# Projection strips in pairs by seven block products, and the last expert pairs loaded by halves

## The reference

```python
proj = x @ w_in + b_in                       # 1024 -> 6 x 1024
ya = (bg * short_conv(cg * xc)) @ w_conv_out
ys = ssm_branch(us)                          # state scan, 64 groups x 64 states
z = gelu(ys)
glu = z * sigmoid(z @ w_glu + b_glu)
yb = glu @ w_ssm_out
m = sigmoid(ga) * ya + sigmoid(gb) * yb
x = layer_norm(ALPHA * x + m @ w_o)
f = moe_ffn(x)       # router: top 8 of 64 experts in 4 of 8 groups; SwiGLU experts of width 256; one shared expert
x = layer_norm(ALPHA * x + f)
```

## Time and profile before

| | us |
|---|---|
| median of 3 runs | 828.49 (826.7 to 829.38) |
| the profiled execution, own time | 828.15 |
| its span on the core | 826.4 |
| PE busy | 807.5 (98%) |
| DVE busy | 465.6 |
| ACT busy | 162.7 |
| POOL busy | 93.2 |
| HBM to and from | 326 GB/s over the span |

### The profile page before, as it was taken

How to read it: one execution, slowest core, us unless ns; L and a number is a source line. 1 busy time by engine, 2 the same in 40 slices (tenths; PEclk the granted TensorE clock), 3 DMA queues, 4 the chain that set the end, 5 groups by cost and what they waited for, 6 DMA issues and landing times.

```text
span 826.4 us, 11871 instructions
## 1 busy us (share of the span) xinstructions
PE 807.5 (98%) x4275; PEld 504.1 (61%) x4275; DVE 465.6 (56%) x1179; ACT 162.7 (20%) x269; POOL 93.2 (11%) x105
## 2 busy tenths in 40 slices
PE   9999999999999999899999999999999999999994
PEld 7876788888788888544445454454545545444442
DVE  6989899999741367534434443343434334334356
ACT  2210112111221005321212112121212112112115
POOL 1119700000010002100000000000000000000021
PEclk9999999999999999999999999999999999999998
DMA  9433344445489946699999999999999999999961
GB/s 330 152 128 103 124 140 144 153 153 114 152 334 420 404 159 268 216 395 418 424 423 420 427 424 420 426 424 421 425 426 422 425 426 422 426 425 423 422 275 54
DMA packets 43639, 262.08 MB, mean 317 GB/s; under 512 B 9736, under 2 KB 10504, under 8 KB 24528
## 3 DMA queue, kind: packets, MB, share of 16 engines
q1 hardware_dynamic: 38992, 252.87, 76.3%
q0 software_dynamic: 4608, 8.66, 2.8%
HBM read 267.10 MB, written 2.53 MB: 326 GB/s over the span
## 4 chain that ended last, share of the span: by engine, by line
PE 83%; DMA 14%; DVE 2%; ACT 1%; issue 0%; SPq 0%; POOL 0%; ACTq 0%; DVEq 0%; POOLq 0%
PE banks L1219 35%; PE banks L1424 22%; DMA ring<-w_gu 14%; PE banks L1467 10%; PE banks L1391 6%; PE banks L1366 3%; PE banks L1320 1%; PE banks L1234 1%; PE banks L1246 1%; PE banks L1396 1%; PE banks L1439 1%; PE banks L1252 1%; PE banks L1495 0%; ACT cgb L697 0%; DVE cgb L1191 0%
## 5 line engine op out<-in xcount | busy, mean ns | idle before, releaser
L1424 PE MATMUL banks<-high,low 128*64 128x512 f32 x848 | 232.1, 593 | 2.2 <-DMA high<-w_gu 2.2
L1219 PE MATMUL banks<-xT,ring 128*128 128x264 f32 x768 | 176.9, 390 | 0.0
L1132 DVE TENSOR_TENSOR cgb<-cgb,banks 128x264 f32<-128x264 f32 x248 | 90.0, 424 | 137.4 <-PE banks L1391 137.3
L1219 PEld LDWEIGHTS banks<-xT,ring 128*128 128x128 f32 x768 | 145.1, 191 | 30.2 <-issue 5.5
L1424 PEld LDWEIGHTS banks<-high,low 128*64 128x64 f32 x848 | 74.2, 137 | 137.2 <-issue 132.4
L1177 DVE SCALAR_TENSOR_TENSOR y_pair<-banks,sml,y_pair 128x1024 fp32r<-128x1024 f32 x31 | 39.8, 1284 | 121.8 <-ACT y_pair L687 121.8
L532 POOL DMA_INDIRECT low<-x_rows_dram,idx x32 | 31.9, 997 | 427.6 <-DVE idx L1076 423.2
L1424 PE MATMUL banks<-ring,low 128*64 128x512 f32 x176 | 77.5, 593 | 1.3 <-DMA ring<-w_gu 1.3
L1391 PEld LDWEIGHTS banks<-sw,y_pair 128*128 128x128 f32 x496 | 63.0, 188 | 24.9 <-issue 24.3
L1467 PE MATMUL banks<-high,mu 128*64 128x512 f32 x336 | 76.7, 598 | 0.2 <-DVE cgb L1132 0.2
L1391 PE MATMUL banks<-sw,y_pair 128*128 128x264 f32 x496 | 71.1, 293 | 0.0
(11 more groups left out here) (294 smaller groups left out, 856.0 us busy)
## 6 DMA issues: line engine op xcount, KB each, us to landing
high<-w_gu SPq DMA_DIRECT2D x40, 2048.0 KB, 28.0
high<-w_dn SPq DMA_DIRECT2D x42, 1024.0 KB, 23.9
ring<-w_front SPq DMA_DIRECT2D x78, 512.0 KB, 3.3
high<-w_gu SPq DMA_DIRECT2D x28, 1024.0 KB, 10.0
ring<-w_gu SPq DMA_DIRECT2D x8, 2048.0 KB, 32.4
us<-w_dn SPq DMA_DIRECT2D x11, 1024.0 KB, 22.5
ring<-w_gu SPq DMA_DIRECT2D x6, 1024.0 KB, 10.4
bgb<-w_dn SPq DMA_DIRECT2D x6, 1024.0 KB, 22.5
```

Of the source, the lines that this page charges most:

```text
L1132: dve.tensor_tensor(acc[:, n], acc[:, n], psum[:, bank, 0:T], ALU.add).then_inc(added, 1)
L1219: ins = pe.matmul(psum[:, 6 + n % 2, 0:T], ring[:, n % RING, k], rhs[:, k], start=(k == 0), stop=(k == KC - 1))
L1424: ins = pe.matmul(psum[SL * j:SL * j + SL, GU_BANK, :], xg[:, k, SL * j:SL * j + SL], gu[slots[j]][:, k], start=(k == 0), stop=(k == KC - 1))
```

## The change

**Pairs of strips by seven products.** The first two GLU strips (0 and 4) stay as they are (`PLAIN`, `FRONT`). The other 22 are done as 11 *quads*: quad q takes strips n and n + 4 of a projection, that is a 2x2 block product: outputs in two chunks, inputs in two groups of four chunks, tokens in two halves of 132. Instead of eight block products it makes seven, of sums and differences of the blocks (Winograd's form). Each is four matmuls of 132 columns. The sums of weight blocks (`left_sums`, four for each quad, 128x512) are made by POOL, those of the activations (`right_sums`, four for each projection) by DVE, and DVE puts the seven products together (`join`), with a first copy by ACT. A quad that begins a projection (3 and 7) takes the first three of four chunks of products 1 to 5 ahead, since the fourth needs the outcome of the quad before.

**DMA.** Quads have three slots of 1 MB, and a pair's strips are one load of two halves; one piece of expert weights stands behind the strips of each of quads 1 to 9. Scratch for the sums lies where expert slots are, so gate and up of experts 0 and 4 and down of expert 5 are no longer loaded between the strips but at the end of the quads, behind the tenth and the eleventh, and the shared expert's down weights at the seventh quad's end.

**Last pairs by halves.** Visit 30 also waits by halves. For visit 31 the second half of gate and up comes in two parts and the down weights by row halves; the combination of visit 30 and the mean move between the two halves of its gate and up matmuls, DVE adds all eight chunks of it before it multiplies the hidden rows (L1161 of before), and the down projection runs over both column halves for each row half.

The core of the diff, for POOL, ACT, and three places of DVE:

```diff
+                for q in range(len(QUADS)):
...
+                    if q > 1:
+                        pool.wait_ge(products, PRODUCTS * (q - 1))
+                    pool.wait_ge(quad_loaded[q % QUAD_RING], 32 * (q // QUAD_RING + 1))
+                    pool.tensor_tensor(s1, two[:, 0:HC], two[:, HC:KC], ALU.add).then_inc(left_ready, 1)
+                    pool.wait_ge(left_ready, 4 * q + 1)
+                    pool.tensor_tensor(s2, s1, one[:, 0:HC], ALU.subtract).then_inc(left_ready, 1)
+                    pool.tensor_tensor(s3, one[:, 0:HC], two[:, 0:HC], ALU.subtract).then_inc(left_ready, 1)
+                    pool.wait_ge(left_ready, 4 * q + 2)
+                    pool.tensor_tensor(s4, one[:, HC:KC], s2, ALU.subtract).then_inc(left_ready, 1)
...
+                for q in range(len(QUADS)):
+                    if q > 1:
+                        act.wait_ge(joined, q - 1)
+                    act.wait_ge(products, PRODUCTS * q + 1)
+                    act.activation(first_product[:, q % 2], psum[:, 3 * (q % 2) + 2, 0:TH], ACT.Copy).then_inc(first_copied, 1)
+                    if q < FIRST_SSM:
+                        act.wait_ge(joined, q + 1)
+                        for c in (q + 1, q + 1 + HC):
+                            glu_gate(c, xcb[:, c]).then_inc(gated, 1)
...
+                def glu_products(i):
+
+                    dve.tensor_tensor(both(cgb, i), both(us, i), both(xcb, i), ALU.mult).then_inc(glu_ready, 1)
+                    dve.wait_ge(glu_ready, i + 1)
+                    if i == HC - 2:
+                        sum_right(1, cgb, 0, HC - 1)
+                    if i == HC - 1:
+                        sum_right(1, cgb, HC - 1, HC)
...
+                for i in range(HC):
+                    if i >= HC - 2:
+                        sum_weights(i - (HC - 2))
+                    join(FIRST_SSM + i, i)
+                    do(dve.tensor_tensor(both(gbb, i), both(xcb, i), both(gbb, i), ALU.mult))
+                    dve.tensor_tensor(both(bgb, i), both(gbb, i), both(bgb, i), ALU.add).then_inc(m_ready, 1)
+                    dve.wait_ge(m_ready, i + 1)
+                    if i == HC - 2:
+                        sum_right(2, bgb, 0, HC - 1)
+                    if i == HC - 1:
+                        sum_right(2, bgb, HC - 1, HC)
...
-                for n in range(KC - 1):
+                for n in READY_ORDER[:KC - 2]:
                     center(0, r_, n)
...
+                join(len(QUADS) - 1, last, xT)
```

More of the change, by code:

```diff
@@ L44 @@
 RING = 4
+PLAIN = GLU + 2
+FRONT = list(range(GLU + 1)) + [GLU + HC]
+QUADS = [GLU + i for i in range(1, HC)] + [SSM + i for i in range(HC)] + [OUT + i for i in range(HC)]
+FIRST_SSM, FIRST_OUT = HC - 1, 2 * HC - 1
+FIRST_QUADS = (FIRST_SSM, FIRST_OUT)
+TH = T // 2
+PRODUCTS, QUAD_RING = 7, 3
+READY_ORDER = [n + HC * h for n in range(HC) for h in range(2)]
 UNIT = 2
@@ L216, in build @@
         strips_done = sem("strips_done")
+        quad_loaded = [sem(f"quad_slot{i}_loaded") for i in range(QUAD_RING)]
+        left_ready = sem("left_sums_ready")
+        right_ready = sem("right_sums_ready")
+        products = sem("quad_products_done")
+        first_copied = sem("quad_first_product_copied")
+        joined = sem("quad_blocks_joined")
+        gated = sem("glu_gates_ready")
         bank_free = [sem(f"bank{i}_free") for i in range(2)]
@@ L693, in _ @@
                 visit(turns * PER_TURN + 1, 1, last=True)
[L694 removed]
+                squares(1, acc, range(KC))
                 for n in range(KC):
@@ L1157, in visit @@
                         dve.wait_ge(added, before + 1)
-                        for n in range(ADDED_FIRST):
+                        for n in range(KC if last else ADDED_FIRST):
                             add(n, before, CHUNK_BANKS[n])
@@ L1161, in visit @@
                     dve.tensor_tensor(h_sl, sil_sl, psum[:, GU_BANK, F:2 * F], ALU.mult).then_inc(hx_ready, 1)
-                    if before is not None:
+                    if before is not None and not last:
                         for n in range(ADDED_FIRST, KC):
@@ L1287, in _ @@
                         pe.wait_ge(mean_parts, 1)
                         pe.matmul(psum[:, MEAN_BANK[0], 0:T], ones[:], mu[:, 2], start=True, stop=True).then_inc(stat_out, 1)
-                    strip(n, bgb, rhs_ready=m_ready if n == OUT else None)
+                    pe.wait_ge(first_copied, q + 1)
+                    pe.wait_ge(left_ready, 4 * q + 4)
+                    product(bank + 2, TH, s4, end[:, HC:KC])
+                    pe.wait_ge(right_ready, 8 * m + 8)
+                    product(bank + 2, 2 * TH, two[:, HC:KC], t4)
@@ L1291, in logits @@
+                for q in range(len(QUADS)):
+                    if q < FIRST_SSM:
+                        quad(q, 0, us)
+                    elif q < FIRST_OUT:
+                        quad(q, 1, cgb, glu_ready)
+                    else:
+                        quad(q, 2, bgb, m_ready)
                 def logits(first, end):
-                    for k in range(first, end):
-                        pe.wait_ge(centered, k + 1)
+                    for i in range(first, end):
+                        k = READY_ORDER[i]
+                        pe.wait_ge(centered, i + 1)
```

310 lines of the change are left out of this document (215 added, 95 removed).

## The result

The changed kernel takes 844.04 us (median of 4 runs, 842.25 to 848.46); the kernel before took 828.93 in the same series (826.7 to 829.4). The ratio is 1.0203, 95% interval 1.0184 to 1.0222: slower by 15 to 18 us, as forecast (845.7). The profiled execution took 844.83, with a span of 843.1, 16.7 more than before.

A forecast was written before the change was run, and what follows sets the result against it. PE was taken to bound the strips (229.5 to 315.6 us), the stream of expert weights the later stage. Terms -9.0 + 21 + 5.4 - 0.3 = +17.1 on the median 828.5 gave 845.7 us with roundings; range 827 to 850.

The forecast's parts named there:

- The bound: Expert stage: the stream of weights bounds it, so the end moves by as much as the first gated load (339.32).
- Products: PE in the quads: 616 matmuls at 0.1125 us replace 22 strips, 69.3 us for 78.3, so -9.0.
- Turns: Quads: POOL's sums and DVE's operations with two SBUF inputs exclude each other for whole operations, making PE wait: +21 us.
- start: First quads: DVE's right sums alternate with POOL's sums, the first join is late and PE waits in quad 1: 7.3 us.
- GLU to SSM: Passage between these projections: right sums alternate with POOL, so third join and product come late for PE: 4.1 us.
- SSM to OUT: Passage between these projections: DVE's multiplications and sums in turns with POOL, then a weight sum, delay PE: 8.4 us.
- sums of inputs: Eight DVE sums of inputs meet POOL's eight router multiplications, so the mean is late: 1.1 us.
- The rival of the clock: PE's clock falls to 1.2 GHz behind each of three pauses, 3 us each: 850 to 854 us; chance 0.07.
- No exclusion: Rival: POOL and DVE hardly hinder each other, sum -4.3, 824.2 us, faster than before; chance 0.13.
- milder: Rival: exclusion on one side only or DVE first, 7 to 15 us instead of 21: 832 to 840; chance 0.24.
- End of the quads: Behind the last quad: DVE's last join and centerings come late and ACT has one more square: +5.4 us.
- Last visits: Visits 30 and 31: visit 30 starts 1.2 to 1.3 us earlier, visit 31 loses 1.0: sum -0.3 us.

The follow-up runs named there:

- run 1: The changed kernel with POOL's 44 sums of weight blocks left out, strip blocks standing in for them: ratio 1.0006 to the kernel before, 828.9 us.
- run 3: A program of its own, without the kernel's computation, with phases of equal POOL and DVE operations alone and together: a pair of two-input sums every 1.55 us.
- Run 9: The kernel before with only the change to visits 30 and 31 (weights by halves, combination and mean moved): ratio 0.9992, 827.6 us.
- run 8: The changed kernel with POOL's five waits, DVE's work reordered, last pair as plain strips, and loads behind the quads in two steps: ratio 0.9994, 827.2 us.

## Why the prediction was right, step by step

- **The bound.** The gated load moved by 16.8 us and the end by 16.7. Right.
- **Products.** 0.1125 a record and 6.30 us a quad: -9.0 as summed. The bounds above it (0.120, 0.129) were not needed. With the 19.2 of the next point, and a start of the strips 0.3 earlier in this execution (229.18 against 229.52), this gives the +9.9 of PE's end.
- **Turns.** Forecast 21, measured 19.2 over a quad's 6.3 and the mean's matmul, at the forecast places: start 7.3 forecast, 7.3 measured (quads 1 and 2); GLU to SSM 4.1 forecast, 2.7 measured; SSM to OUT 8.4 and 8.9, with 0.3 more in quad 6; sums of inputs 1.1 and nothing. But this agreement is in part luck. A pair of operations costs 1.55 us, not the 1.85 that I put together from whole lengths, so the first join ended at 250.6 and not 253.6 and PE's pause was 4.4 and not 6.2; the first wait of 1.1 for right sums did not come (quad 0 takes 6.4). What filled the term up again is the clock: about 2.6 us in quads 1 and 2 and 2.0 in quad 7 are records at 0.22 us, behind the pauses. So half clock made 4.6 and waiting some 14.6, where the sum had 21 for waiting alone; and of the 14.6 the 2.1 of run 1 are there without POOL, so they are DVE's own backlog and not the turns.
- **The rival of the clock** I priced at 3 us a pause and took for unlikely (0.07). It was the case at all three long pauses, with 2.0 to 2.6 us each; as it came with smaller pauses the time stayed near the forecast. The step that failed is treating turns and clock as alternatives: the forecast was right in what makes the time, and the clock, 7.0 us in all, was missing from the sum.
- **The other rivals.** *No exclusion* falls by runs 1 and 3, *milder* by run 3, where the sums go strictly one after the other. The rule of the Trainium skill (SBUF — State Buffer, "Who interferes with whom") holds in the phases shown in run 3; by it an operation in a two-port mode contends too, which fits the one-input operation in one piece. POOL's operation with one input, in the last section, is where the measurement differs from it.
- **End of the quads.** Forecast 5.4, measured 6.9. The last chunks are ready 4.7 us behind PE's end instead of 0.5, so 4.2 later, where 5.1 was forecast. The second square is 0.3, as forecast. The other 2.4 is half clock until the matmuls of the logits are done, which the sum did not have.
- **Last visits.** Forecast -0.3; in the changed kernel visit 30 starts 1.2 us earlier against the stream (797.05 against 781.52, +15.5), the last down projection 0.6 later (823.03 against 805.69, +17.3), and the end is -0.1. Run 9 agrees.
- **Value without the turns.** I gave 824.2; run 1 shows 828.9. Had POOL and DVE not met, the change would have been no gain: the wait in quad 7 is 2.1 us and not 1.3, and the half clock behind it and behind the last quad (2 and 2.4 us) was not in the sum.

## What to carry to other kernels

A helper engine with idle time is not a free place for work: first look which of its operands and of DVE's lie in SBUF. Where they meet, let the one with slack wait at the few critical places (five waits gave 12.5 us), shorten its operations (6 us), or give DVE an operand in PSUM, which only the program of run 3 and the joins show. And price a pause of PE with what comes behind it: 4 to 6 us of waiting cost another 2 to 2.6 here. An earlier router was worth little here, once the transfers had been moved into its way.

## What the runs showed of the hardware

- POOL with a one-input operation of 128x512 (1.49 us alone) blocks DVE's two-input sum only in part. In its phase (groups of run 3) twelve sums take 7.5 us, a mean of 699 ns, and POOL's own 1807. Of DVE's sums every third takes 0.97 to 1.02 us and the two behind it 0.56, so no turn is as long as POOL's operation.

```profile
L116 POOL TENSOR_SCALAR pool_out<-pool_a 128x512 f32<-128x512 f32 x5 | 8.9, 1807 | 0.1
L120 DVE TENSOR_TENSOR dve_out<-dve_a,dve_b 128x396 f32<-128x396 f32 x12 | 7.5, 699 | 1.6 <-POOL pool_out L115 1.6
```

- A wait of PE of 2.07 us (run 1, quad 7) was followed by records at half speed; waits of 1.64 and 0.88 us close together in run 8 were not (granted clock 1.00 from 282 to 300 us). In the run with plain last strips, waits of 1.6 and 1.0 us in quad 3 were followed by eight records in 1.78 us instead of 1.06; the changed kernel, with 1.2 and 1.0, had none. What decides it these runs don't show.
- The long reduction of DVE (128x2112, one input) ran at 4.03 us beside POOL, as alone (3.99 in the earlier trace rows), and held POOL up as little.
